# Rotary scores of latent attention in three reduced-precision products, and half-sized projection units in the sparse attention

## The chip, the cores and the metric

The program runs on one core of a Trainium2 chip. Times are device microseconds (us) from the start to the end of one execution. TensorE (PE, with its weight loads as PEld) does the matrix products, VectorE (DVE) and ScalarE (ACT) work on tiles of 128 partitions by 512 elements in on-chip memory, GpSimd (POOL) prepares weights, SyncE (SP) issues weight loads. The metric is the time of the whole program; lower is better.

## The reference

One input x (1 x 512 x 1024, float32) goes through two blocks. Only what the change touches is cut out here: the latent attention (MLA) of the first block and the sparse attention of the second.

```
q = (c_q @ w_uq).reshape(bsz, seq, 16, 128 + 64)          # MLA: c_q has 256 columns
q_rope = apply_rope(q[..., 128:], cos, sin)
k_rope = apply_rope(ckr[..., 256:], cos, sin)               # one for all heads
apply_rope: [x1 * cos - x2 * sin, x2 * cos + x1 * sin]      # halves of 32
s = einsum(q_nope, k_nope) + einsum(q_rope, k_rope); softmax(s * scale, causal) @ v

proj = h @ w_in                                             # second block
q_lat = einsum("bshd,hdc->bshc", q, w_uk)                   # 16 heads
att_lat = softmax(q_lat . c_kv * scale + bias, selected keys) @ c_kv
att = einsum("bshc,hdc->bshd", att_lat, w_uv)
xbc = silu(causal_depthwise_conv(xbc, w, b))                # 4 taps
z * silu(z); sigmoid(g_att), sigmoid(g_ssm)
```

## The kernel before, in words

Everything is held transposed: features on partitions, the 512 positions along the free axis. A projection is a sum over 128x128 weight blocks. For near-float32 precision at the fast rate each operand is split into a rounded part "hi" and a rest "lo" of type fp32r, and `product` (L505 to L512) issues three matmuls of 128x512: hi x hi, hi x lo, lo x hi. Plain f32 matmuls are used where no split was made. The weights come in 376 tiles of eight blocks each, in the order in which PE uses them. Per tile SP loads the raw tile, POOL loads a rounded copy (L439) and subtracts (`w_lo`, L457), both some tiles ahead, and PE tells by `slots_free` that it began a tile.

Each engine has its own program, written out in order; semaphores join them. There is no planner: the tables at the top of the file set the order.

**MLA.** `kv` computes four tiles of 128 features (two of latent, one of rotary keys, one of the same keys with the halves of 32 swapped). Then come "units", each one bank of PSUM (bank 6 or 7 in turn): `d` (query latent, 24 matmuls), and for each of four groups of four heads `k`, `v`, `q` (6 matmuls each, four of each kind) and `r`: four per group, two with rotary queries and two with the swapped ones. For a pair of heads DVE multiplies the one by the cosine and the other by the sine and adds (L2062, L2065, L2067). The first group's units run ahead of the loop. The loop has 64 items, one per head and block i of 128 queries, with (i+1) x 128 keys. Per step n PE makes the scores of item n (L950: nope part, f32, 128 rows; L951: rotary part, f32, 64 rows; L952: causal mask, fp32r), at n = 6, 10, ... the product of probabilities and values of a head (L964, f32), the transposes of item n-2 (L979), and then the next group's units that `GROUP_STEPS` gives for n mod 16. DVE takes the row maximum of item n (L2101, L2103), normalises item n-1 (L2108, L2110), then frees its units. ACT takes the exponential (L1454), copies transposes (L1462), and rounds head outputs (L1442). Scores use banks 0 to 2, transposes 3 and 4, head outputs 5.

**Sparse attention.** Again 64 items. PE makes scores (L1117 f32, L1118 to L1120 fp32r), head products (L1127), transposes (L1142), and in each step the units of `D_STEPS[n]`: 44 large projections of 24 matmuls each (4 `gs`, 16 `z`, 24 `xb`), and small ones: `ql` (next head's latent query, L1015) and `uv` (values of two heads, L1019). All of them take banks 6 and 7 in turn; a unit waits until the one two before it was read. An `xb` unit is a convolution: ACT writes the last tap (L1504), DVE adds three more (L2138) and, a unit later, multiplies with the tanh (L2151); `z` needs ACT's tanh (L1500) and one DVE step (L2131). DVE does this at the end of the same step n, before the row maximum of item n+1. Results are stored to DRAM ("spilled") and read back in the state-space stage that follows, which starts with transposes (L1203), `products` into bank 5 (L1189), and on ACT with a wait for all stores before the gate tiles are loaded (L1638); DVE multiplies with them (L2179) and then scales the next transposed tile (L2395).

The places that the diff touches:

## Time and profile before

| | |
|---|---|
| time, median of 3 runs (lowest, highest) | 2756.27 us (2754.8, 2764.29) |
| the profiled execution's own time | 2756.11 us |
| its span, first to last instruction | 2754.2 us |
| PE busy | 2622.4 us (95%), 11724 matmuls |
| DVE, ACT, POOL busy | 1467.7 us (53%), 657.5 us (24%), 1139.1 us (41%) |
| mean granted clock of TensorE | 0.978 of 2.4 GHz |
| weight traffic | 436.62 MB moved, 159 GB/s mean |

A matmul's duration includes its fill, and neighbours overlap: 128x512 fp32r matmuls show some 0.39 us each, but start every 0.23 us. So the cost of PE work is read from start to start, and "busy" counts nearly all of the span. MLA's loop runs from 769.5 to about 1004 us, the sparse attention's from 1626 to 2051 us, the state-space stage after that. The profile's own times are some 2 us under the time of the execution.

### The profile page before, as it was taken

The numbers are of one execution on the slowest core, as the hardware profiler recorded it, in microseconds if no ns is written. First come the engines' busy times: TensorE is split into PE (matmuls) and PEld (weight loads), VectorE is DVE, ScalarE is ACT, GpSimd is POOL, SyncE is SP. The second block draws the span as 40 slices with busy tenths as digits, with TensorE's granted clock in tenths as the row PEclk, the third lists the DMA queues.
The fourth block names the chain that finished last, engine by engine and source line by source line (L and its number), as shares of the span: only waits on it lengthen the run. The fifth ranks groups of instructions, "written<-read, shape, count | busy, mean of one in ns | idle before, by whom it ended". The sixth has DMA issues, their size and how long they took to land.

```text
span 2754.2 us, 31018 instructions
## 1 busy us (share of the span) xinstructions
PE 2622.4 (95%) x11724; PEld 2045.0 (74%) x11724; DVE 1467.7 (53%) x2001; ACT 657.5 (24%) x1289; POOL 1139.1 (41%) x764
## 2 busy tenths in 40 slices
PE   7999899999999999999999999999989998899998
PEld 6888688888766668888886676766666666688886
DVE  4754574464644434645556774454445777555511
ACT  2003430021323321201113213332222431222200
POOL 4333355555421125555554443333222224455554
PEclk9999999999989999999999999999999999999999
DMA  6333356555421225555654564444353535456564
GB/s 204 123 116 125 121 190 198 188 194 194 158 77 62 65 85 189 197 189 193 209 189 152 156 224 136 157 149 139 129 183 123 168 96 175 144 193 198 186 197 168
DMA packets 149049, 436.62 MB, mean 159 GB/s; under 512 B 14064, under 2 KB 18352, under 8 KB 148912
## 3 DMA queue, kind: packets, MB, share of 16 engines
q1 hardware_dynamic: 64224, 200.29, 24.7%
q0 software_dynamic: 67584, 201.35, 20.9%
q10 hardware_dynamic: 17104, 33.14, 3.5%
q8 instruction: 88, 1.44, 0.2%
q14 instruction: 49, 0.40, 0.0%
HBM read 417.90 MB, written 16.83 MB: 158 GB/s over the span
## 4 chain that ended last, share of the span: by engine, by line
issue 36%; PE 33%; POOL 24%; DVE 3%; DMA 2%; ACT 2%; DVEq 1%; ACTq 0%; POOLq 0%; SPq 0%
POOL w_lo L457 19%; PE bank L509 9%; PE bank L512 9%; PE bank L511 9%; POOL w_hi L439 5%; PE bank L710 2%; DMA projections<-spill_out 1%; PE bank L1127 1%; PE bank L784 1%; DMA residual<-x_in 0%; PE bank L787 0%; PE bank L786 0%; PE bank L1087 0%; DVE next_gained L2273 0%; PE bank L1117 0%
## 5 line engine op out<-in xcount | busy, mean ns | idle before, releaser
L457 POOL TENSOR_TENSOR w_lo<-w_raw,w_hi 128x1024 fp32r<-128x1024 f32 x376 | 905.7, 2409 | 14.8 <-DMA w_hi<-stream 6.5
L439 POOL DMA_DIRECT2D w_hi<-stream x376 | 227.2, 604 | 1582.7 <-PE bank L509 1413.8
L509 PE MATMUL bank<-x_hi,w_hi 128*128 128x512 f32 x1472 | 590.2, 401 | 26.0 <-POOL w_lo L457 13.0
L511 PE MATMUL bank<-x_lo,w_hi 128*128 128x512 f32 x1472 | 578.4, 393 | 0.0
L512 PE MATMUL bank<-x_hi,w_lo 128*128 128x512 f32 x1472 | 577.8, 393 | 0.0
L509 PEld LDWEIGHTS bank<-x_hi,w_hi 128*128 128x128 f32 x1472 | 279.6, 190 | 94.8 <-issue 20.4
L512 PEld LDWEIGHTS bank<-x_hi,w_lo 128*128 128x128 f32 x1472 | 279.4, 190 | 59.5
L511 PEld LDWEIGHTS bank<-x_lo,w_hi 128*128 128x128 f32 x1472 | 279.7, 190 | 57.8 <-issue 2.4
L2010 DVE TENSOR_TENSOR relu_sq<-relu 128x512 f32<-128x512 f32 x64 | 179.1, 2799 | 94.6 <-ACT relu L1404 94.6
L509 PE MATMUL bank<-hidden_hi,w_hi 128*128 128x512 f32 x512 | 199.2, 389 | 0.0
L511 PE MATMUL bank<-hidden_lo,w_hi 128*128 128x512 f32 x512 | 199.2, 389 | 0.0
L512 PE MATMUL bank<-hidden_hi,w_lo 128*128 128x512 f32 x512 | 199.2, 389 | 0.0
L1404 ACT ACTIVATE relu<-bank 128x512 f32<-128x512 f32 x64 | 38.3, 599 | 404.8 <-PE bank L512 404.8
L2138 DVE SCALAR_TENSOR_TENSOR conv_acc<-bank,half_conv,conv_acc 128x511 f32<-128x511 f32 (+2 forms) x72 | 53.9, 748 | 112.0 <-ACT conv_acc L1504 107.9
L511 PEld LDWEIGHTS bank<-hidden_lo,w_hi 128*128 128x128 f32 x512 | 96.1, 188 | 20.1
L509 PEld LDWEIGHTS bank<-hidden_hi,w_hi 128*128 128x128 f32 x512 | 96.1, 188 | 20.1
L512 PEld LDWEIGHTS bank<-hidden_hi,w_lo 128*128 128x128 f32 x512 | 96.1, 188 | 19.6
L509 PE MATMUL bank<-x_mlp_hi,w_hi 128*128 128x512 f32 x256 | 100.1, 391 | 0.6 <-POOL w_lo L457 0.6
L512 PE MATMUL bank<-x_mlp_hi,w_lo 128*128 128x512 f32 x256 | 99.6, 389 | 0.0
L511 PE MATMUL bank<-x_mlp_lo,w_hi 128*128 128x512 f32 x256 | 99.6, 389 | 0.0
L2483 DVE SCALAR_TENSOR_TENSOR ffn_val<-bank,consts,ffn_val 128x511 f32<-128x511 f32 (+1 forms) x44 | 33.0, 749 | 86.4 <-ACT ffn_val L1757 84.8
L2021 DVE TENSOR_TENSOR mlp_scaled<-bank,mlp_rstd 128x512 f32<-128x512 f32 x16 | 11.1, 692 | 110.0 <-PE bank L512 110.0
(434 smaller groups left out, 4448.4 us busy)
## 6 DMA issues: line engine op xcount, KB each, us to landing
w_hi<-stream POOLq DMA_DIRECT2D x376, 512.0 KB, 4.7
w_raw<-stream SPq DMA_DIRECT2D x376, 512.0 KB, 3.7
projections<-spill_out ACTq DMA_DIRECT2D x56, 256.0 KB, 2.0
ssm_x<-projections ACTq DMA_DIRECT2D x4, 1024.0 KB, 7.5
gate_tiles<-projections ACTq DMA_DIRECT2D x16, 256.0 KB, 3.6
ssm_z<-projections ACTq DMA_DIRECT2D x16, 256.0 KB, 2.7
residual<-x_in SPq DMA_DIRECT2D x4, 512.0 KB, 11.6
toeplitz_hi<-toeplitz_rows_hi POOLq DMA_DIRECT2D x4, 512.0 KB, 6.6
```

Of the source, the lines that this page charges most:

```text
L439: e.dma_start(in_slot(whi, t % SLOTS, o), in_stream(o)).then_inc(hi_ready[t % SLOTS], 16)
L457: e.tensor_tensor(wlo[:, s, :], raw[:, s, :], whi[:, s, :].bitcast(F32), ALU.subtract).then_inc(lo_ready, 1)
L509: mm = e.matmul(out, wh, rh, start=first, stop=False)
L511: e.matmul(out, wh, rl, start=False, stop=False)
L512: return e.matmul(out, wl, rh, start=False, stop=last)
L710: mm = e.matmul(o.rearrange("p (n l) -> p n l", l=L), hks[:, hh, chunk(c)], right, start=True, stop=True)
L784: mm = e.matmul(o, xh[:, k, chunk(t)], wh, start=k == 0, stop=False)
L1127: mm = e.matmul(bank[5][:, k * P:], dcn[:, k, :], mpt[:, k, k * P:], start=k == 0, stop=k == ST - 1)
L1404: e.activation(r_[:, j, :], bank[j][:, :], ACT.Relu).then_inc(f.free, 1)
L2010: tt(t_[:, j, :], r_[:, j, :], r_[:, j, :], ALU.mult)
L2138: mm = stt(a[:, lag:S], b[:, 0:S - lag], half_conv[:, 24 * k + m:24 * k + m + 1], a[:, lag:S], ALU.mult, ALU.add)
L2483: mm = stt(acc[:, lag:S], b[:, 0:S - lag], weights[:, 44 * k + t:44 * k + t + 1], acc[:, lag:S], ALU.mult, ALU.add)
```

## The change

In MLA the swapped weights are no longer used: `kv` has three tiles, and a group has two `r` units. DVE makes the swap itself by reading other partitions, in four operations on 32 partitions (`rotated`), adds, and the sum is split into hi (ACT) and lo (DVE). Keys are split likewise, once, with a mask so that each half of 64 partitions has its own pair of tiles whose other half is zero. The rotary score is three fp32r matmuls over 128 rows in place of one f32 matmul over 64. `GROUP_STEPS` changes.

In the sparse attention a large unit is issued in two halves of 12 matmuls (`half_unit`), spread over the steps by `D_PARTS`; DVE handles a unit one step after ACT. `ql` and `uv` move to bank 5, in an order given by `FIFTH`, and `products` waits until bank 5 was read. The last two large units are now convolutions, in steps 64 and 66; they were `z` units in steps 66 and 67.

```
-for _k, _u in enumerate(_mixed):
-    D_STEPS[_k * D_ITEMS // len(_mixed)].append(_u)
-D_STEPS[66].append(("z", 0, 14))
-D_STEPS[67].append(("z", 0, 15))
-for _h in range(1, 16):
-    D_STEPS[4 * _h - 3].append(("ql", 0, _h))
-for _t in range(8):
-    D_STEPS[8 * _t + 12].append(("uv", 0, _t))
+_halves = [(_u, _kh) for _u in _mixed for _kh in range(2)]
+for _n in range(D_ITEMS):
+    D_PARTS[_n] = [_halves.pop(0) for _ in range(2 if _n % 4 == 0 or _n % 16 == 11 else 1)]
+D_PARTS[D_ITEMS] = [_halves.pop(0) for _ in range(2)]
+D_PARTS[D_ITEMS + 2] = _halves
+for _n, _parts in enumerate(D_PARTS):
+    D_STEPS[_n] = [_u for _u, _kh in _parts if _kh]
+UV_AT = {8 * _t + (12 if _t < 7 else 11): _t for _t in range(8)}
+QL_AT = {4 * _h - 3: _h for _h in range(1, 16)}
...
+FIFTH = []
+for _n in range(len(D_STEPS)):
+    if _n >= 6 and _n % 4 == 2:
+        FIFTH.append(("out", _n // 4 - 1))
+    if _n in UV_AT:
+        FIFTH.append(("uv", UV_AT[_n]))
+    if _n in QL_AT:
+        FIFTH.append(("ql", QL_AT[_n]))
+FIFTH_AT = {_x: _n for _n, _x in enumerate(FIFTH)}
...
-        rp, kr = at("rope_table", 200, [P, 2, S]), at("mla_k_rope", 204, [P, S])
+        rp, rsum = at("rope_table", 200, [P, 2, S]), at("rope_sum", 130, [P, S])
+        krh = [at(f"mla_k_rope_hi{x}", kb, [P, S], F32R) for x, kb in enumerate((204, 134))]
+        krl = [at(f"mla_k_rope_lo{x}", kb, [P, S], F32R) for x, kb in enumerate((132, 136))]
...
-            UNITS += [(_k, 0, _j) for _j in range(4)]
-        GROUP_STEPS = {2: ["v0"], 3: ["v1"], 4: ["v2"], 5: ["v3"], 6: ["k0", "k1"], 7: ["k2", "k3"], 8: ["q0"],
-                       9: ["q1"], 10: ["q2"], 11: ["q3"], 12: ["r0", "r1"], 13: ["r2"], 14: ["r3"]}
+            UNITS += [(_k, 0, _j) for _j in range(2 if _k == "r" else 4)]
+        GROUP_STEPS = {3: ["v0"], 4: ["v1", "v2"], 5: ["v3"], 7: ["k0"], 8: ["k1", "k2"], 9: ["k3", "q0"], 11: ["q1"],
+                       12: ["q2", "q3"], 13: ["r0"], 15: ["r1"]}
...
-                        s, m = r_slot[0], (0, 2, 1, 3)[j]
+                        s = r_slot[0]
                         for k in range(2):
-                            b = slice((2 * m + k) * P, (2 * m + k + 1) * P)
+                            b = slice((2 * j + k) * P, (2 * j + k + 1) * P)
...
+                    if n % 8 == 0:
+                        e.wait_ge(rope_done, 2 + n // 8 + 1)
+                    if g and n % 16 == 0:
+                        e.wait_ge(un_act, 4 * (2 * g - 1))
                     if n >= 3:
                         e.wait_ge(at_e, n - 2)
                     b, w_ = bank[n % 3], (i + 1) * P
-                    r = slice(64 * (j % 2), 64 * (j % 2) + 64)
+                    x = rope_slot(n // 8)
+                    qh, ql, kh, kl = rqh[x][:, chunk(i)], rql[x][:, chunk(i)], krh[j % 2][:, 0:w_], krl[j % 2][:, 0:w_]
                     e.matmul(b[:, 0:w_], gq[g % 2][:, j, chunk(i)], gk[g % 2][:, j, 0:w_], start=True, stop=False)
-                    e.matmul(b[:, 0:w_], gr[g % 2][r, j // 2, chunk(i)], kr[r, 0:w_], start=False, stop=False)
+                    e.matmul(b[:, 0:w_], qh, kh, start=False, stop=False)
+                    e.matmul(b[:, 0:w_], ql, kh, start=False, stop=False)
+                    e.matmul(b[:, 0:w_], qh, kl, start=False, stop=False)
...
+            def half_unit(u, kh):
+
+                _, _, j = UNITS[u]
+                o = bank[6 + u % 2]
+                if kh == 0:
+                    a, d = freed_before(u - 1)
+                    if by_act(u - 2):
+                        e.wait_ge(un_act, a)
+                    else:
+                        e.wait_ge(un_dve, d)
+                for k in range(4 * kh, 4 * kh + 4):
+                    mm = product(e, w, o[:, :], xh2[:, k, :], xl2[:, k, :], k == 0, k == 7)
+                if kh:
+                    mm.then_inc(un_full, 1)
...
+                def head_values(t):
+                    e.wait_ge(at_oc, FIFTH_AT["uv", t])
+                    for q in range(2):
+                        mm = e.matmul(bank[5][64 * q:64 * q + 64, :], wuv[:, 2 * t + q, :], dlo[:, q, :],
+                                      start=True, stop=True)
+                    mm.then_inc(at_o, 1)
+
+                def next_query(hh):
+                    e.wait_ge(at_oc, FIFTH_AT["ql", hh])
+                    latent_query(bank[5][:, :], hh).then_inc(at_o, 1)
...
-                    for x in D_STEPS[n]:
-                        unit(UNIT_AT[x])
+                    if n in UV_AT:
+                        head_values(UV_AT[n])
+                    if n in QL_AT:
+                        next_query(QL_AT[n])
+                    for x, kh in D_PARTS[n]:
+                        half_unit(UNIT_AT[x], kh)
...
+                        e.wait_ge(at_oc, len(FIFTH))
                         products(0)
...
+                def rope_high(pair):
+                    e.wait_ge(rope_full, 1 + pair + 1)
+                    e.activation(rqh[rope_slot(pair)][:, :], rsum[:, :], ACT.Copy).then_inc(rope_hi, 1)
...
+                        rotated(rsum[:, :], rt[:, :], b).then_inc(un_dve, 1)
                         e.drain()
-                        tt(o, rt[:, :], o, ALU.add).then_inc(rope_done, 1)
-                        e.drain()
+                        tt(rsum[:, :], rt[:, :], rsum[:, :], ALU.add).then_inc(rope_full, 1)
+
+                def rotated(o, own, x):
+                    tt(own, x, rp[:, 0, :], ALU.mult)
+                    for q in range(4):
+                        a, b = slice(32 * q, 32 * q + 32), slice(32 * (q ^ 1), 32 * (q ^ 1) + 32)
+                        mm = tt(o[a], x[b], rp[b, 1, :], ALU.mult)
+                    return mm
+
+                def rope_low(pair):
+                    x = rope_slot(pair)
+                    e.wait_ge(rope_hi, 2 + pair + 1)
+                    tt(rql[x][:, :], rsum[:, :], rqh[x][:, :].bitcast(F32), ALU.subtract).then_inc(rope_done, 1)
+                    e.drain()
...
-                for u in range(6, 18):
+                for x in range(2):
+                    e.wait_ge(rope_hi, x + 1)
+                    stt(krl[x][:, :], krr[:, 1, :], own_half[:, x:x + 1], krh[x][:, :].bitcast(F32), ALU.mult,
+                        ALU.subtract).then_inc(rope_done, 1)
+                for u in range(6, 16):
                     unit(u)
+                    if u >= 14:
+                        rope_low(u - 14)
+                low_next = None
                 for n in range(MLA_ITEMS + 2):
                     if n < MLA_ITEMS:
...
-                    for x in D_STEPS[n]:
+                    if n in UV_AT:
+                        t = UV_AT[n]
+                        e.wait_ge(uv_hi, t + 1)
+                        tt(atl[:, t, :], bank[5][:, :], ath[:, t, :].bitcast(F32), ALU.subtract).then_inc(at_oc, 1)
+                        e.drain().then_inc(at_lo, 1)
+                    for x in (D_STEPS[n - 1] if n else []):
                         unit(UNIT_AT[x])
+                for x in D_STEPS[-1]:
+                    unit(UNIT_AT[x])
```

DVE in MLA's loop, second group's rotary units, before: the last product waits a step, and a rotary pair is three operations (`mla_o_lo` is a head output's lo part).

```order
L2062 TENSOR_TENSOR rope_tmp<-bank,rope_table 128x512
L2101 TENSOR_REDUCE mla_row_max<-bank 128x1
L2103 TENSOR_SCALAR mla_neg_max<-mla_row_max 128x1
L2108 RECIPROCAL mla_row_inv<-mla_row_sum 128x1
L2110 TENSOR_SCALAR mla_probs<-mla_probs,mla_row_inv 128x256
L2065 TENSOR_TENSOR mla_gq_rope_107<-bank,rope_table 128x512
L2067 TENSOR_TENSOR mla_gq_rope_107<-rope_tmp,mla_gq_rope_107 128x512
L2072 TENSOR_TENSOR mla_o_lo<-bank,mla_o_hi 128x512
```

After, at the same place (step 15 and 16):

```order
L2132 TENSOR_TENSOR rope_tmp<-bank,rope_table 128x512
L2135 TENSOR_TENSOR rope_sum<-bank,rope_table 32x512 x4
L2129 TENSOR_TENSOR rope_sum<-rope_tmp,rope_sum 128x512
L2186 TENSOR_REDUCE mla_row_max<-bank 128x1
L2188 TENSOR_SCALAR mla_neg_max<-mla_row_max 128x1
L2193 RECIPROCAL mla_row_inv<-mla_row_sum 128x1
L2195 TENSOR_SCALAR mla_probs<-mla_probs,mla_row_inv 128x512
L2141 TENSOR_TENSOR mla_rope_lo_111<-rope_sum,mla_rope_hi_108 128x512
```

What was spread over two steps as three operations of 128 partitions stands now in one block of six, ahead of the next row maximum, with a seventh behind it.

DVE from the last normalised item to the state-space stage (`ssm_x_nat`, `merged`), before:

```order
L2330 RECIPROCAL mla_row_inv<-mla_row_sum 128x1
L2332 TENSOR_SCALAR mla_probs<-mla_probs,mla_row_inv 128x512
L2131 SCALAR_TENSOR_TENSOR spill_out<-tanh_175,bank 128x512
L2151 SCALAR_TENSOR_TENSOR spill_out<-tanh_176,conv_acc 128x512
L2131 SCALAR_TENSOR_TENSOR spill_out<-tanh_176,bank 128x512
L2174 TENSOR_TENSOR att_lo<-bank,att_hi 128x512
L2395 TENSOR_TENSOR ssm_x_nat_196<-bank,ssm_dt 128x512
L2179 SCALAR_TENSOR_TENSOR merged<-gate_tiles,bank 128x512
```

After:

```order
L2228 SCALAR_TENSOR_TENSOR conv_acc<-bank,half_conv,conv_acc 128x509
L2241 SCALAR_TENSOR_TENSOR spill_out<-tanh_185,conv_acc 128x512
L2422 TENSOR_TENSOR att_lo<-bank,att_hi 128x512
L2228 SCALAR_TENSOR_TENSOR conv_acc<-bank,half_conv,conv_acc 128x511
L2228 SCALAR_TENSOR_TENSOR conv_acc<-bank,half_conv,conv_acc 128x510
L2228 SCALAR_TENSOR_TENSOR conv_acc<-bank,half_conv,conv_acc 128x509
L2241 SCALAR_TENSOR_TENSOR spill_out<-tanh_184,conv_acc 128x512
L2241 SCALAR_TENSOR_TENSOR spill_out<-tanh_185,conv_acc 128x512
L2488 TENSOR_TENSOR ssm_x_nat_205<-bank,ssm_dt 128x512
L2265 SCALAR_TENSOR_TENSOR merged<-gate_tiles,bank 128x512
```

The last operations ahead of `ssm_x_nat` were one each for two `z` units and a tanh product; now a convolution's three taps and two tanh products stand there, behind the last `att_lo`.

## Rows read from the trace of the kernel before

**Rows 1.** Busy time by stretch: span, engines' busy (count), clock, DMA.
```profile
1050.00:1100.00 50.00, 50.00 (x223) 41.39 (x221) 23.68 (x16) 7.50 (x11) 27.50 (x18) 1.00 0.60 189
...
770.90:794.80 23.90, 23.90 (x51) 11.92 (x50) 6.74 (x26) 5.76 (x19) 0.00 (x0) 0.50 0.00 0
...
1626.00:2051.00 425.00, 393.35 (x1724) 294.82 (x1724) 191.42 (x374) 124.61 (x300) 134.10 (x92) 0.97 0.45 145
```

**Rows 2.** PE's waits from 735 to 1010 us: total us, times, longest.
```profile
PE bank L893 <- DVE mla_gv L2058: 4.1, 1, 4.1
PE bank L979 <- DVE mla_probs L2110: 4.0, 7, 1.3
PE bank L950 <- DVE mla_gq_rope L2067: 1.6, 1, 1.6
```

**Rows 3.** PE's waits from 1626 to 2051 us.
```profile
PE bank L1142 <- DVE mla_probs L2332: 23.0, 10, 4.1
PE bank L1127 <- ACT mla_probs_t L1608: 6.6, 6, 3.2
```

**Rows 4.** Timeline of PE in MLA: start, duration, line, operation.
```profile
870.65 2.37 PE L964 MATMUL bank<-mla_probs_t,mla_gv 128*128 128x512 f32 x8
...
874.36 1.02 PE L950 MATMUL bank<-mla_gk,mla_gq 128*128 128x512 f32 x2
...
876.53 0.40 PE L979 MATMUL bank<-consts,mla_probs 128*128 128x128 f32 x2
876.69 0.48 PE L509 MATMUL bank<-mla_cq_hi,w_hi 128*128 128x512 f32 x1
877.01 0.39 PE L511 MATMUL bank<-mla_cq_lo,w_hi 128*128 128x512 f32 x1
...
878.17 0.38 PE L950 MATMUL bank<-mla_gk,mla_gq 128*128 128x128 f32 x2
...
879.06 0.51 PE L979 MATMUL bank<-consts,mla_probs 128*128 128x128 f32 x3
```

**Rows 5.** Timeline of PE in the sparse attention, no unit between.
```profile
1767.76 1.02 PE L1117 MATMUL bank<-dsa_c,dsa_qlat 128*128 128x512 f32 x2
...
1768.85 0.28 PE L1119 MATMUL bank<-toeplitz_hi,flip_r 128*128 128x256 f32 x1
...
1769.31 0.39 PE L1117 MATMUL bank<-dsa_c,dsa_qlat 128*128 128x128 f32 x2
...
1769.59 0.28 PE L1119 MATMUL bank<-toeplitz_hi,flip_r 128*128 128x128 f32 x1
1769.70 0.28 PE L1120 MATMUL bank<-toeplitz_lo,flip_r 128*128 128x128 f32 x1
```

**Rows 6.** DVE's groups of instructions by shape: busy us, mean ns.
```profile
L2249 DVE TENSOR_TENSOR ssm_acum_t_lo<-bank,ssm_acum_t_hi 32x512 fp32r<-32x512 f32 x1 | 0.7, 669 | 0.0
```

**Rows 7.** ACT's copy of a head output in MLA, same view.
```profile
L1442 ACT ACTIVATE mla_o_hi<-bank 128x512 fp32r<-128x512 f32 x16 | 9.5, 592 | 4.1 <-PE bank L964 4.1
```

**Rows 8.** Timeline of DVE, MLA's loop and the state-space stage.
```profile
876.73 0.69 DVE L2101 TENSOR_REDUCE mla_row_max<-bank 128x1 f32<-128x512 f32 x1 [0.88 <-PE bank L952]
...
877.80 0.42 DVE L2110 TENSOR_SCALAR mla_probs<-mla_probs,mla_row_inv 128x384 f32<-128x384 f32 x1
...
2085.34 1.29 DVE L2387 TENSOR_TENSOR ssm_g<-bank,ssm_g 128x512 f32<-128x512 f32 x2 [2.95 <-ACT ssm_g L1663]
```

**Rows 9.** Timeline: a DVE operation beside POOL's `w_lo`.
```profile
1999.34 2.87 DVE L2332 TENSOR_SCALAR mla_probs<-mla_probs,mla_row_inv 128x384 f32<-128x384 f32 x1
1999.57 2.40 POOL L457 TENSOR_TENSOR w_lo<-w_raw,w_hi 128x1024 fp32r<-128x1024 f32 x1
```

**Rows 10.** Timeline: end of the sparse attention and start of the state-space stage.
```profile
2050.96 1.08 PE L1019 MATMUL bank<-dsa_lat,dsa_wuv 128*64 128x512 f32 x4
...
2059.92 0.69 DVE L2179 SCALAR_TENSOR_TENSOR merged<-gate_tiles,bank 128x512 f32<-128x512 f32 x1 [5.61 <-DMA gate_tiles<-projections]
...
2061.49 0.66 PE L1203 MATMUL bank<-consts,ssm_x 128*128 128x128 f32 x4 [2.04 <-DVE ssm_x_nat L2395]
```

More of the change, by code:

```diff
@@ L85 @@
 D_ITEMS = 64
-D_STEPS = [[] for _ in range(D_ITEMS + 5)]
+D_STEPS = [[] for _ in range(D_ITEMS + 4)]
+D_PARTS = [[] for _ in D_STEPS]
 _others = [("gs", 0, m) for m in range(4, 8)] + [("z", 0, m) for m in range(16)]
@@ L146 @@
 for _g in (2, 3):
-    _x = [x for us in D_STEPS[16 * _g - 15:] for x in us if x[0] in SECTION][0]
+    _x = [x for parts in D_PARTS[16 * _g - 15:] for x, kh in parts if kh == 0][0]
     BIAS_AT[FETCH_AT[FIRST[SECTION[_x[0]]] + _x[2], None]] = [_g]
@@ L914, in mla @@
                 for kh in range(2):
-                    for m in range(4):
+                    for m in range(3):
                         if kh == 0:
-                            e.wait_ge(*(f.ring[m] if m < 4 else (f.free, f.f0 + m - 3)))
+                            e.wait_ge(*f.ring[m])
                         for k in range(4 * kh, 4 * kh + 4):
@@ L936, in mla @@
                 e.wait_ge(la_lo, 4)
-                for u in range(10, 18):
+                for u in range(10, 16):
                     unit(u)
@@ L996, in _, with latent_query @@
             mlp(1)
+            def latent_query(o, j):
+                r = slice(64 * (j % 2), 64 * (j % 2) + 64)
+                return e.matmul(o, wuk[r, j // 2, :], dq2[r, j // 2, :], start=True, stop=True)
+            def half_unit(u, kh):
[11 more added lines that the diff above has]
+                    mm.then_inc(un_full, 1)
             def unit(u):
@@ L1010, in unit @@
                 elif kind == "ql":
[L1011 to L1020 removed]
+                    e.wait_ge(extra_loaded, 16 * 5)
+                    e.wait_ge(un_act, freed_before(UNIT_AT["dq", 0, 7] + 1)[0])
+                    mm = latent_query(o[:, :], j)
                 elif kind == "ys":
@@ L1123, in out_product @@
                     e.wait_ge(at_c, n0 + 4 * hh + 4)
[L1124 to L1125 removed]
+                    e.wait_ge(at_oc, FIFTH_AT["out", hh])
                     for k in range(ST):
@@ L1447, in mla @@
                 latent(1, cq, cqh, rstd_q)
+                e.wait_ge(rope_full, 1)
+                for x in range(2):
+                    e.activation(krh[x][:, :], krr[:, 1, :], ACT.Copy, scale=own_half[:, x:x + 1]).then_inc(rope_hi, 1)
+                for pair in range(2):
+                    rope_high(pair)
                 for n in range(MLA_ITEMS + 2):
```

91 lines of the change are left out of this document (44 added, 47 removed), and 2 rows, old and new, of the table flow.

## The prediction

> **What bounds the kernel now.** I read the page first (PE busy 95%, the other engines at most 53%), then the stretches, then PE's waits in the two stages that change, then single steps in the timeline. The reader is to see that PE is the bound nearly everywhere, so two things count: PE's work, and the pauses and slow stretches of PE. In dense work a 128x512 matmul starts every 50 / 223 = 0.224 us at the full clock of 2.4 GHz [rows 1]. In MLA PE hardly waits inside the loop: 4.0 us in seven pauses, and in the run-up 4.1 and 1.6 us [rows 2]. But from 770.9 to 794.8 us, right behind the 1.6 us pause, the granted clock is 0.50, the 1.2 GHz level, while PE makes only scores, transposes and a head product; with the first dense units it is back [rows 1]. In the sparse attention PE waits 23.0 us for normalised rows, which DVE makes late because it had a convolution first, and 6.6 us for copied transposes [rows 3]; the mean clock there is 0.97 over 425 us [rows 1].
>
> **MLA, PE's work.** `kv` loses one tile of 24 matmuls, each group two `r` units of 6, in all 24 + 48 = 72, times 0.224 = -16.1 us [rows 1]. PE follows the chain of DVE there, but the first wait of that chain (`nx_sum`) is earlier than the work removed, so I count all of it. (If DVE held PE, 5 us of it would go.)
>
> A score item takes now 876.53 - 874.36 = 2.17 us at 512 keys and 879.06 - 878.17 = 0.89 at 128 [rows 4]; the widths between lie on a line, so a head costs 2 x (2.17 + 0.89) = 6.12. After: f32 plus one fp32r matmul take 1768.85 - 1767.76 = 1.09 at 512 and 1769.59 - 1769.31 = 0.28 at 128, a fp32r one 0.224 at 512 and 1769.70 - 1769.59 = 0.11 at 128 [rows 1, 5]. With two more fp32r and the mask (0.11) an item is 1.09 + 0.45 + 0.11 = 1.65 and 0.28 + 0.22 + 0.11 = 0.61, a head 4.52. That saves 1.6 per head, 16 heads, -25.6 us. The three matmuls cost less than the one since f32 takes about four times as long per column and the 64-row weights load in the open. The first seven items run at half clock, where the saving (seven quarters of 1.6 us) counts twice: -2.8 us. Bounds for the scores: -15 us, if only the f32 matmul goes and each fp32r one costs its width plus its weight load, to -31 us.
>
> **MLA, what DVE adds.** A `rotated` block is five products, a sum and the lo part. An operation on 32 partitions lasts 669 ns [rows 6], as long as one on 128: its price follows the free size. Back to back, two start 1.29 - 0.69 = 0.60 apart [rows 8]. So from the end of the `r` unit: 4 x 0.60 + 0.69, a drain of 0.1, the sum 0.69: 3.9 us; then ACT 0.59 [rows 7] and the lo part 0.69, with 0.1 for each hand-over: 5.4 us. In the run-up PE has for the first pair only the second `r` unit (6 x 0.224 = 1.35 us) to do, so it pauses 4.2 us where it was 1.6 [rows 2]: +2.6. The keys' two lo parts stand ahead of the values that release PE: 2 x 0.69, +1.4 behind the 4.1 us pause.
>
> In the loop the queue behind a `rotated` block is what hurts. Step 13 (`r0`) is followed by a head product of 2.2 us [rows 4] and two wide items, which cover it. Step 15 (`r1`) is followed by short work: items 0 and 1 of the next head, 0.6 and 0.9 us, with some 0.3 of transposes. DVE begins `r1` late, because row maximum, normalising and a head's lo part of step 14 came first: PE waits about 0.7 us in step 16. Then 3.9 us of rotation, and from row maximum to normalised row another 1.2 (at 512 wide it is 877.80 + 0.42 - 876.73 = 1.49 [rows 8]), while PE has 1.3 us: about 3.7 us of pause in step 17, and 0.8 for the copy behind it. 5.2 us a group, three groups: +15.6 us. Bounds: 0, if the operations overlap better, to 27, if the lo part counts too. In steps without dense work the shorter score also uncovers DVE's 1.49 us [rows 8]: +0.5 per head for four heads, +2.
>
> **MLA, the clock.** A pause of 1.6 us among f32 work was followed by 23.9 us at 0.50 [rows 1, 2]. The new 3.7 us pauses lie in steps 16 to 18 that have no dense units; the next is in step 19. I expect 5 to 7 us at half clock at each, 3 us lost, +9 for three. From 0 (no fall) to 30 (fall until the dense work of several steps has passed).
>
> Sum for MLA: -16.1 - 25.6 - 2.8 + 2.6 + 1.4 + 15.6 + 2 + 9 = -13.9 us.
>
> **Sparse attention.** No matmul goes. What goes is the pause: with half a unit (12 x 0.224 = 2.7 us) in every step and DVE a step later with the taps, the normalised row that PE transposes in step n is made before the convolution of step n-1, with some 8 us of PE work between. Of 23.0 + 6.6 us [rows 3] I leave 4 (a tail of 0.7, the rest where POOL stalls DVE): -25.6. The clock: 0.03 x 425 = 12.8 us' worth of ticks [rows 1], of which a few fall into pauses; I take -9. The 24 or so additional changes between kinds of matmul cost 877.01 - 876.69 - 0.224 = 0.1 us each [rows 4]: +2.5. `ql` and `uv` have each other's readers to wait for in bank 5, steps apart and behind a half unit: 0 to +4, taken 0.
>
> The seam to the state-space stage gets worse. Now `uv`, at 2050.96, is followed at 2059.92 by the first product with a gate tile and at 2061.49 by the transposes that wait for DVE behind it, a pause of 2.0 us [rows 10]. Afterwards `products` waits for ACT's and DVE's reading of bank 5 (0.6 + 0.7), and the last large unit is a convolution: three taps (2.4), tanh (0.6), the product (0.7), all behind `att_lo`, before its store, and the gate's load waits for that store on ACT. That moves 2059.92 by some 5.5 us. `products`, the dense unit and the first transposes cover none of it, since they are in the 2.0 us pause's calculation already: +5.5, and +2.5 for a fall of the clock in a pause of over 6 us. Bounds 2 and 14.
>
> Sum: -25.6 - 9 + 2.5 + 5.5 + 2.5 = -24.1 us. All: -38.0 from the profiled 2756.11, so 2718.1; the median 2756.27 lies 0.2 above the profile, and I say 2718.
>
> **A rule against the change.** A DVE operation that lasts 0.42 us elsewhere took 2.87 when POOL's 2.40 us `w_lo` began beside it [rows 8, 9]. The rotation's sums and lo parts read two tiles from on-chip memory; the products read PSUM. The Trainium skill, SBUF — State Buffer, section "Who interferes with whom", says that a DVE instruction with two SBUF inputs contends with a GpSimd instruction that reads SBUF, and that the one issued second is blocked until the other ends; the one row here is of a form with one tensor and a column, and it agrees in size.
>
> **The rivals.** (1) The port: POOL starts a `w_lo` about when a new weight tile is begun, and each group's `r0` begins one. If it fell on the sum or lo part of both blocks, 2 x 2.4 us for three groups and the run-up: +19, so 2737. Against it: the five products come first and last 3.1 us, longer than a `w_lo` of 2.40 [rows 9] that begins beside them, and each reads PSUM, as the 1.29 us pair does [rows 8]. By the skill's rule, too, they would pass beside it. (2) The new DVE blocks and half clock eat MLA's gain whole: the upper bounds of pauses and clock (27 and 30 in place of 15.6 and 9), MLA +18, total 2750; a milder form 2735. For it: MLA's DVE had no such block, and the 23.9 us row. (3) The pauses in MLA don't come (PE's work covers the blocks): 15.6 + 9 less, 2693. (4) The lag does not do what it says: the halves let PE reach a transpose sooner after a score, and DVE with stalls from POOL is late all the same; half of the 30 us stays with its clock, +18: 2736. (5) Slower: the clock falls in MLA and stays. Place: the loop from 795 to 1004 us; mechanism: pauses of over 3 us in work that, as the 23.9 us row shows, does not bring 2.4 GHz back; price: half of each us spent so. It decides from 2 x 52 us on, half of the loop, since 38 + 14 must be lost: 2775. Against it: dense units stand in ten of 16 steps, and with dense work the clock came back at once.
>
> **How the numbers follow.** Chances: forecast 0.48, (3) 0.17, (2) 0.15, (1) 0.09, (4) 0.07, (5) 0.04. 0.5% is 13.8 us, about what a measurement of this kernel can tell from no change. Faster than 2742.5 are the forecast, (3), (1), (4) nearly whole, and the milder half of (2): 0.87. Same 0.09, slower 0.04. The range from 2692 to 2741 takes in (3), (1), (4) and the milder (2), and leaves 0.15 out; the forecast's own is 2705 to 2730.
>
> **What would show it.** PE matmuls +56 (128 more, 72 fewer). MLA items of about 1.65 and 0.61 us. In MLA three pauses of 3 to 4 us before transposes (waiting for `mla_probs`) in the second step of each of the last three groups, with clock 0.50 behind them. In the sparse attention the waits of 23.0 and 6.6 us fall below 5 in sum, and the clock stays above 0.99. A pause of about 6 us before the second transposes of the state-space stage. Wrong would be: pauses left in the sparse attention, an operation on 32 partitions that lasts well off 0.67 us, or a fp32r matmul of 128 columns over 0.15 us.

## The result and the profile after

The change made the kernel faster: 2723.95 us (median of 4 runs, 2719.7 to 2730.51) against 2756.25 for the kernel before beside it. The ratio is 0.9878, with a 95% interval from 0.9865 to 0.9891: 33.6 us less by the ratio, 32.3 by the medians. The forecast was 2718. The profiled execution took 2719.7 (span 2717.9); it was the fastest of the four. The total fits, but not by the forecast's terms: MLA gave back nearly everything, the sparse attention gave more. First the two stages of the kernel before, by busy time between the same two instructions (first MLA score to first product with `mla_o_hi`; first sparse score to `products`); then the same of the changed kernel. Columns: stretch, its length, PE busy (count), PEld, DVE, ACT, POOL, mean granted clock, DMA share, GB/s.

```profile
769.51:1006.97 237.46, 232.76 (x897) 143.32 (x897) 100.77 (x301) 83.18 (x231) 35.45 (x24) 0.94 0.17 54
1626.14:2052.46 426.32, 394.81 (x1730) 295.47 (x1731) 192.11 (x375) 125.49 (x301) 134.10 (x92) 0.97 0.44 145
```

```profile
767.66:1005.00 237.34, 203.41 (x924) 155.01 (x925) 135.47 (x332) 87.11 (x238) 35.23 (x24) 0.91 0.17 54
1623.25:2013.19 389.94, 383.14 (x1731) 290.82 (x1731) 173.13 (x371) 124.89 (x300) 133.64 (x92) 1.00 0.49 159
```

MLA's loop lasts as long as before, though PE is busy 29 us less in it. Length less busy is idle: 4.7 us before, 33.9 after. Busy multiplied by the clock is the work at 2.4 GHz, to some 2 us, since the clock has two digits: 219 before, 185 after. So 34 us of work went, 29 us of pauses and 4 us of half clock came. In the sparse attention the work is some 383 us in both; 24.7 us of pauses went, and busy time fell by 11.7, to all appearance the slow clock's.

PE's waits of the changed kernel, first from 700 to 1010 us (they answer to [rows 2]), then from 1626 to 2051 (to [rows 3]): total us, times, longest.

```profile
PE bank L1001 <- DVE mla_probs L2195: 32.8, 21, 4.0
PE bank L910 <- DVE mla_gv L2123: 5.4, 1, 5.4
PE bank L970 <- DVE mla_rope_lo L2141: 4.4, 1, 4.4
PE bank L522 <- POOL w_lo L470: 1.9, 2, 1.0
...
PE bank L1254 <- DVE ssm_x_nat L2488: 6.1, 2, 5.3
PE bank L1189 <- DVE mla_probs L2418: 3.3, 6, 0.6
...
PE bank L1163 <- ACT mla_probs_t L1666: 1.4, 1, 1.4
```

MLA's transposes wait for normalised rows 21 times, 32.8 us, where it was 4.0 in seven; the sparse ones 3.3 where it was 23.0. Now the timeline of one group's turn in MLA, in order of time; in brackets what the engine idled before the row, and for whom.

```profile
822.15 0.69 DVE L2132 TENSOR_TENSOR rope_tmp<-bank,rope_table 128x512 f32<-128x512 f32 x1
...
822.85 2.79 DVE L2135 TENSOR_TENSOR rope_sum<-bank,rope_table 32x512 f32<-32x512 f32 x4
...
825.73 0.69 DVE L2129 TENSOR_TENSOR rope_sum<-rope_tmp,rope_sum 128x512 f32<-128x512 f32 x1
...
827.12 0.49 DVE L2195 TENSOR_SCALAR mla_probs<-mla_probs,mla_row_inv 128x512 f32<-128x512 f32 x1
...
827.66 1.11 PE L1001 MATMUL bank<-consts,mla_probs 128*128 128x128 f32 x4 [3.98 <-DVE mla_probs L2195]
...
834.18 1.02 PE L970 MATMUL bank<-mla_gk,mla_gq 128*128 128x512 f32 x2
...
835.80 0.39 PE L1001 MATMUL bank<-consts,mla_probs 128*128 128x128 f32 x2
...
837.07 2.83 DVE L2195 TENSOR_SCALAR mla_probs<-mla_probs,mla_row_inv 128x384 f32<-128x384 f32 x1
...
837.31 2.36 POOL L470 TENSOR_TENSOR w_lo<-w_raw,w_hi 128x1024 fp32r<-128x1024 f32 x1
...
839.96 0.55 PE L1001 MATMUL bank<-consts,mla_probs 128*128 128x128 f32 x3 [1.76 <-DVE mla_probs L2195]
```

The rotation takes 4.27 us, and PE pauses 3.98 behind it, as forecast (3.7). A score item of 512 keys takes 835.80 - 834.18 = 1.62 us (forecast 1.65, before 2.17 [rows 4]). What the forecast did not have is the last part: a normalising that [rows 8] show at 0.42 us takes 2.83 beside POOL's `w_lo`, and PE pauses 1.76 us. That happens six times in MLA (791.47, 839.96, 855.09, 901.69, 916.82 and 965.76 us). A third thing that no term of the forecast names stands at the loop's start: the second pair's rotation lies ahead of the loop's first row maxima, and PE pauses 2.72 us.

```profile
772.68 0.69 DVE L2141 TENSOR_TENSOR mla_rope_lo<-rope_sum,mla_rope_hi 128x512 fp32r<-128x512 f32 x1 [0.70 <-ACT mla_rope_hi L1498]
773.46 0.29 DVE L2186 TENSOR_REDUCE mla_row_max<-bank 128x1 f32<-128x128 f32 x1
...
775.09 0.48 PE L1001 MATMUL bank<-consts,mla_probs 128*128 128x128 f32 x1 [2.72 <-DVE mla_probs L2195]
```

The long normalising never came in MLA before; one line's own view of each kernel shows the longest of 64 at 491 ns before and at 2835 ns after (min, median, max):

```profile
L2110 DVE TENSOR_SCALAR mla_probs<-mla_probs,mla_row_inv x64: 285/387/491, 773.7 to 1001.4; 128x128 f32<-128x128 f32 x16, 128x256 f32<-128x256 f32 x16, 128x384 f32<-128x384 f32 x16, 128x512 f32<-128x512 f32 x16
```

```profile
L2195 DVE TENSOR_SCALAR mla_probs<-mla_probs,mla_row_inv x64: 285/386/2835, 774.8 to 998.8; 128x128 f32<-128x128 f32 x16, 128x256 f32<-128x256 f32 x16, 128x384 f32<-128x384 f32 x16, 128x512 f32<-128x512 f32 x16
```

The cause was looked for in `GROUP_STEPS`: the tiles of `v` and `k` are now begun in steps 3 and 7 of a group, where DVE normalises 384 columns at the moment when POOL starts on the next tile. The experiment with the units one to a step tries this.

### The profile page after: what moved, and what is told of

It is laid out like the page before. It is cut to its first block, busy times and chain, and to the rows that moved or that the text cites. A ratio compares the mean times of both kernels' runs of the same rounds, so it can differ in the third digit from the quotient of the medians.

```text
span 2717.9 us, 31048 instructions
## 1 busy us (share of the span) xinstructions
PE 2571.4 (95%) x11716; PEld 2044.5 (75%) x11716; DVE 1495.3 (55%) x2046; ACT 663.1 (24%) x1299; POOL 1134.9 (42%) x764
## 4 chain that ended last, share of the span: by engine, by line
issue 35%; PE 33%; POOL 24%; DVE 4%; DMA 2%; ACT 2%; DVEq 1%; ACTq 0%; POOLq 0%; SPq 0%
POOL w_lo L470 19%; PE bank L522 9%; PE bank L525 8%; PE bank L524 8%; POOL w_hi L452 5%; PE bank L727 2%; DMA projections<-spill_out 1%; PE bank L1154 1%; PE bank L1163 1%; DMA residual<-x_in 1%; PE bank L801 1%; PE bank L804 0%; PE bank L803 0%; PE bank L1121 0%; DVE next_gained L2359 0%
## 5 line engine op out<-in xcount | busy, mean ns | idle before, releaser
L522 PE MATMUL bank<-x_hi,w_hi 128*128 128x512 f32 x1464 | 587.8, 402 | 28.8 <-POOL w_lo L470 15.3
L522 PEld LDWEIGHTS bank<-x_hi,w_hi 128*128 128x128 f32 x1464 | 276.7, 189 | 113.8 <-issue 40.4
L522 PE MATMUL bank<-hidden_hi,w_hi 128*128 128x512 f32 x512 | 199.3, 389 | 0.0
L2409 DVE TENSOR_REDUCE mla_row_max<-bank 128x1 f32<-128x128 f32 (+1 forms) x64 | 31.4, 491 | 183.4 <-PE bank L1157 182.5
L522 PEld LDWEIGHTS bank<-hidden_hi,w_hi 128*128 128x128 f32 x512 | 96.2, 188 | 19.8
L522 PE MATMUL bank<-x_mlp_hi,w_hi 128*128 128x512 f32 x256 | 100.2, 391 | 0.6 <-POOL w_lo L470 0.6
```

The lines of the kernel that those rows point to most:

```text
L522: mm = e.matmul(out, wh, rh, start=first, stop=False)
L2409: e.reduce_max(mmx[:, n:n + 1], bank[n % 3][:, 0:wd], axis=AX.X)
```

## The experiments

Times are compared with runs of the kernel before on the same chip, in five rounds each. Executions of one kernel differ by some us, so where a few us matter I read the same stretch in both profiles.

**Each half alone.** The kernel before with only the MLA edits, and with only the sparse edits.

> The kernel before with the MLA half of the change alone (rotary scores in hi and lo, kv with three tiles, two r units, new group steps); the sparse attention is the old one. Theory A (MLA's matmul work did shrink by some 40 us, but PE pauses behind DVE and half clock give nearly all of it back): 1 to 5 us faster than before, 2752 to 2755; MLA shows the same pauses as in the changed kernel (three of 4.0 us, six of 1.76 us), the sparse attention its old pauses of 30 us. Rival B (the MLA half alone gains some 14 us, as forecast, and the traces of before and after differ by luck of the clock): 2742. Rival C (it has no effect on the rest but the halves of the change work together): time outside the sum of the two parts by over 5 us.

> The kernel before with the sparse half of the change alone (halved units, DVE's taps a step later, uv and ql in the fifth bank). Theory A (nearly the whole gain is here): 29 to 32 us faster, 2724 to 2727, with pauses of about 7 us in the stage and one of 5.3 us at the seam. Rival B (sparse part gains the 24 forecast): 2732. The two halves' gains should sum to that of the whole change within 3 us.

MLA alone: 2764.68 us, ratio 1.0027 (1.0016 to 1.0038), slower by 4 to 10 us. Sparse alone: 2727.02, 0.9888 (0.9873 to 0.9903), 31 us faster. So all of the gain is the sparse half's, and theory A holds for the two stages: in the first kernel MLA's loop lasts 237.38 us with the very pauses of the changed kernel, and its sparse stage has the old ones.

```profile
766.98:1004.36 237.38, 203.46 (x924) 154.87 (x925) 135.42 (x332) 87.21 (x238) 35.22 (x24) 0.91 0.17 54
1627.09:2055.67 428.58, 396.78 (x1731) 297.38 (x1731) 192.51 (x375) 125.31 (x301) 133.98 (x92) 0.97 0.44 144
```

But the two do not sum to the whole within the 3 us expected: +7.4 - 30.9 = -23.5 us, and the whole change has -33.6, so rival C's sign (off by over 5 us) came. Theory A expected MLA alone 1 to 5 us faster, which is a miss. Its profiled execution, 2756.99 us, was the fastest of its seven, so the profile doesn't show what the median holds. These 10 us stay open. The profiles show one thing that can make such differences without any edit: stages whose code is the same differ by some us from profile to profile, with the granted clock. The part behind the first product with `ssm_xd` in the changed kernel, and in the second kernel of the last group of experiments:

```profile
2036.93:2717.89 680.96, 637.26 (x2906) 494.39 (x2906) 373.90 (x464) 170.59 (x328) 291.17 (x192) 0.98 0.52 165
```

```profile
2012.40:2698.15 685.75, 642.36 (x2906) 497.14 (x2906) 374.03 (x464) 170.57 (x328) 291.84 (x192) 0.97 0.51 164
```

So a stage is compared with the same stage, and a few us of the total are not laid to an edit.

**The rotation block of `r1` a step later on DVE, and its hi part a step later on ACT.** PE makes the unit where it did. DVE's edit (ACT's is of the same kind):

```
-  for u in STEP_UNITS[n]:                      # DVE, end of step n
+  for u in (r1 of STEP_UNITS[n - 1]) + (STEP_UNITS[n] without r1):
```

> The changed kernel with one thing moved in MLA: the rotation block of each group's second r unit is made by DVE one step later, behind the normalising of item 15 of the group (and ACT's hi part of it a step later). Same instructions. Theory A (the 3.98 us pause in the group's step 17 is the rotation block of 4.3 us standing ahead of the normalising): the three pauses fall below 1.5 us each and the half clock behind them goes: 3 x (2.5 to 4) + 3 x 2 = 12 to 18 us faster than the changed kernel, about 2708. Rival B (the block only moves: the next transposes wait as long, as head product and one item do not cover it): no gain, 2720 to 2725. Rival D (clock gives nothing back, since 0.5 us pauses and the 1.76 us ones keep it low): 8 to 10 us, 2714.

2728.29 us, ratio 0.9894 (0.9879 to 0.9909): no gain. Rival B's mechanism is right; the time lies 3 us above its range. PE's, DVE's and ACT's timeline around a group's start:

```profile
826.50 2.79 DVE L2138 TENSOR_TENSOR rope_sum<-bank,rope_table 32x512 f32<-32x512 f32 x4
...
829.38 0.69 DVE L2132 TENSOR_TENSOR rope_sum<-rope_tmp,rope_sum 128x512 f32<-128x512 f32 x1
...
830.11 0.63 ACT L1498 ACTIVATE mla_rope_hi<-rope_sum 128x512 fp32r<-128x512 f32 x1 [3.99 <-DVE rope_sum L2132]
...
830.79 0.47 ACT L1515 ACTIVATE mla_probs<-bank,mla_neg_max 128x256 f32<-128x256 f32 x1
...
831.26 0.59 ACT L1523 ACTIVATE mla_probs_t<-bank 128x512 f32<-128x512 f32 x1
...
831.90 2.02 PE L986 MATMUL bank<-mla_probs_t,mla_gv 128*128 128x512 f32 x2 [3.94 <-ACT mla_probs_t L1523]
```

The transposes no longer wait, but ACT's hi part of the rotated row waits for DVE, and behind it in ACT's queue stands the copy that the head product needs. The pause of 3.98 us became one of 3.94. (An expectation further down says that the block was moved on DVE alone; ACT's part was moved with it.)

**Units one to a step.** Here only the table differs:

```
-  {3: [v0], 4: [v1, v2], 5: [v3], 7: [k0], 8: [k1, k2], 9: [k3, q0], 11: [q1], 12: [q2, q3], 13: [r0], 15: [r1]}
+  {2: [v0], 3: [v1], 4: [v2], 5: [v3], 6: [k0], 7: [k1], 8: [k2], 9: [k3], 10: [q0], 11: [q1], 12: [q2, q3], 13: [r0], 15: [r1]}
```

> The changed kernel with MLA's dense units placed one to a step from step 2 on, so that the weight tiles of v, k and q are begun in steps 2, 6 and 10 of a group in place of 3, 7 and 9; r0 and r1 stay at 13 and 15. Same instructions. Theory A (the 1.76 us pauses are DVE's normalising of 384 columns, blocked for 2.4 us by POOL's lo part of a tile begun in the same step): all six go with the six blocked rows of 2.83 us, 10.6 us of pause and 1 to 4 us of clock less; single units in steps 4 and 8 may bring up to 0.7 us each back (4.5 us): 2710 to 2718. Rival B (the pauses come from the short distance between score and transposes in steps 4 and 8 and have nothing to do with POOL): they stay or grow, since those steps now have half the dense work: 2722 to 2735.

2707.86 us, ratio 0.9822 (0.9808 to 0.9835), 16 us below the changed kernel. All six blocked rows and all six pauses of 1.76 us are gone, and no other pause came; that is theory A, and 2 us more than its range:

```profile
769.96:990.88 220.92, 197.57 (x924) 150.97 (x925) 120.76 (x332) 87.06 (x238) 35.50 (x24) 0.93 0.18 58
```

```profile
L2195 DVE TENSOR_SCALAR mla_probs<-mla_probs,mla_row_inv x64: 285/386/491, 777.0 to 984.5; 128x128 f32<-128x128 f32 x16, 128x256 f32<-128x256 f32 x16, 128x384 f32<-128x384 f32 x16, 128x512 f32<-128x512 f32 x16
```

The loop is 237.34 - 220.92 = 16.4 us shorter: idle 33.9 to 23.3, which is six times 1.76, and the rest is clock. This settles POOL's `w_lo` beside the normalising as the cause, with DVE as the one that waits. The runs show the wait, and not the place where the two meet; that it is a port is the reading given further down.

**The second `r` unit in the next group's step 1**, in addition to the table above:

```
-  15: [r1]
+  1: [r1 of this group, not of the next]
```

> The kernel with units one to a step (v, k, q begun in steps 2, 6, 10 of a group), and here each group's second r unit is moved, on PE, ACT and DVE alike, from step 15 to step 1 of the next group, in front of a head product and a dense unit; it is needed only eight items into the group. In the changed kernel with the block one step later on DVE alone, the pause of 3.98 us had turned into one of 3.94 us of the head product for ACT's copied transposes, since ACT's hi part of the rotated row waits ahead of that copy. Theory A (a rotation block needs some 5.4 us of PE work between it and the transposes or product that come next, whichever engine's queue they stand in; step 1 has 1.2 + 2.2 + 1.3 + 1.6 us): the three pauses of 3.98 us go and nothing over 1 us takes their place; 9 to 12 us of pause and up to 6 of half clock less than with the units one to a step: 2690 to 2699. Rival B (the pause moves a second time, to the copy or the head product of step 18): 2704 to 2708.

2700.91 us, ratio 0.9802 (0.9788 to 0.9815). The loop lasts 213.05 us (220.92 with r1 in step 15). The three pauses of 3.98 us are gone; apart from the 2.7 us at the loop's start, PE's longest are now 1.50 us. Idle is 18.0 us against 23.3. The time lies between theory A's range and rival B's. Theory A's direction holds, but it promised 9 to 12 us of pause and I got 5.3: 1.50 us appear in step 16 of a group, where no dense unit is left ahead, and 0.7 and 0.3 behind the unit's new place.

**The sparse half, taken apart.** Without the lag; with whole units (42 over 64 steps; the expectation's 38 is wrong); and with neither, so that the fifth bank stays, and with it the two convolutions at the end.

```
no lag:        -  for x in D_STEPS[n - 1]: unit(x)     +  for x in D_STEPS[n]: unit(x)
whole units:   -  D_PARTS[n] = one or two halves       +  D_PARTS[k * 64 // 42] += both halves of unit k
```

> The changed kernel, but DVE makes the taps of a sparse-attention unit in the step in which PE ends it, not one step later; halves stay. Theory A (the lag is what takes the normalising out from behind the taps; the halves only spread the work): the normalised rows are late again in steps with a convolution, 12 to 24 pauses of 0.5 to 1.5 us: 10 to 20 us slower than the changed kernel, 2734 to 2744. Rival B (the halves alone do it, since half a unit of PE work stands in every step, and the lag is of no account): 2720 to 2727.

> The changed kernel with the sparse attention's dense units whole again (38 whole units over 64 steps, one or none to a step, as before; the last two are convolutions in steps 64 and 66), with the lag and the fifth bank kept. Theory A (the lag does most; whole units leave steps with no dense work, where DVE's row maximum and normalising, 1.5 us, and its stalls by POOL are uncovered): pauses of 12 to 20 us in place of 6.8: 5 to 13 us slower, 2729 to 2737. Rival B (the halves do it all, the lag nothing): the old pauses come back, 25 to 30 us: 2745 or more.

> The changed kernel with both the lag and the halves undone in the sparse attention: whole units, taps in the step in which PE ends the unit; only uv and ql in the fifth bank stay of that half of the change. The runs so far: halves without the lag have the same 0.55 us pauses as the changed kernel, whole units with the lag 0.85 us ones. Theory A (either of the two is enough, since each puts a half or a whole unit of PE work, 2.7 to 5.4 us, between the taps and the transposes that need the row behind them): with neither, the old pauses of 1.5 to 4 us come back, 20 to 30 us in the stage with its clock: 2745 to 2756. Rival B (the fifth bank did it: uv and ql no longer stand in the ring of two banks behind the taps, and lag and halves add little): pauses of 8 to 13 us, 2725 to 2735.

No lag: 2724.30 us, ratio 0.9878 (0.9862 to 0.9893), the same as with it. Whole units: 2733.41, 0.9917 (0.9903 to 0.9930). Neither: 2778.98, 1.0080 (1.0065 to 1.0096), slower than the kernel before by 22 us. The stage up to `products` in that order of kernels, one fence each:

```profile
1628.81:2021.30 392.49, 384.51 (x1730) 291.86 (x1730) 194.81 (x375) 124.58 (x301) 133.65 (x92) 1.00 0.48 158
```

```profile
1623.66:2017.52 393.86, 384.88 (x1730) 291.88 (x1730) 187.71 (x371) 124.85 (x300) 134.11 (x92) 1.00 0.47 157
```

```profile
1622.80:2069.05 446.25, 405.38 (x1730) 303.82 (x1730) 185.20 (x375) 124.94 (x301) 133.88 (x92) 0.95 0.42 139
```

389.9 with both, 392.5 and 393.9 with one, 446.3 with neither: against the old pauses either edit is enough. Theory A of the first of these runs, that the lag does the work, fell. The whole units came out in theory A's range, 9 us above the changed kernel, but with 9.0 us of idle time in the stage in place of the 12 to 20 expected; the profiles put 4 us in the stage, 1 in the seam and 5 in the last, unchanged stage, so what the halves are worth beside the lag is between 4 and 9 us. Theory A of the last run held, and my price for it was too low. DVE's normalising is blocked by POOL even more often without the lag (20 rows, 8 with it; 25 and 11 with the products with a tanh), but the half unit in each step covers it. The kernel to compare the last run with is the MLA-only one, which has the same MLA and the old sparse attention (2764.68 us, stage 428.6). Why the kernel with neither is 14 us slower than that (idle time of the stage 40.9 us for 31.8) stands in its waits, and in ACT's and DVE's timeline before the longest wait for `dsa_qlat`:

```profile
PE bank L1188 <- DVE mla_probs L2417: 23.8, 11, 4.0
PE bank L1162 <- ACT dsa_qlat L1680: 7.7, 5, 2.6
PE bank L1162 <- ACT mla_probs_t L1665: 4.3, 2, 2.9
```

```profile
1857.26 2.40 DVE L2227 SCALAR_TENSOR_TENSOR conv_acc<-bank,half_conv,conv_acc 128x511 f32<-128x511 f32 x3 [1.89 <-ACT conv_acc L1566]
...
1860.84 0.47 ACT L1657 ACTIVATE mla_probs<-bank,mla_neg_max 128x256 f32<-128x256 f32 x1 [3.61 <-DVE mla_neg_max L2410]
...
1861.78 0.60 ACT L1680 ACTIVATE dsa_qlat<-bank 128x512 f32<-128x512 f32 x1
```

The old 23 us are back, and the head product in bank 5 now waits too for ACT's reading of `ql`, which stands in ACT's queue behind exponentials that wait for DVE's taps. The fifth bank alone, with the new end, is a loss; the halves or the lag pay for it.

**Two `z` units last.**

```
+  for _z in (14, 15): _mixed.remove(("z", 0, _z)); _mixed.append(("z", 0, _z))
```

> The changed kernel with the order of the sparse attention's dense units changed at its end: the two z units 14 and 15 come last in place of two convolutions (as before the change), so that the last unit needs one tanh and one product of DVE and no taps. Theory A (the 5.3 us pause before the state-space stage's transposes is the taps of the last convolution, which stand behind the last head's lo part and ahead of the store that the gate's load waits for): the pause falls to 2 to 3 us: 2 to 4 us faster, 2716 to 2722. Rival B (the wait is for products that need bank 5's readers, and the order of units is of no account): 2721 to 2726 and a pause of 5 us.

2724.49 us, ratio 0.9884 (0.9869 to 0.9899): by the total nothing. The place itself: the pause at the second transposes is 2.39 us (first row below), it was 5.31 (the rows of the changed kernel behind it).

```profile
2031.55 0.66 PE L1257 MATMUL bank<-consts,ssm_x 128*128 128x128 f32 x4 [2.39 <-DVE ssm_x_nat L2491]
```

```profile
2013.19 1.16 PE L1240 MATMUL bank<-ssm_c,ssm_b 128*128 128x128 f32 x8 [1.00 <-DVE att_lo L2422]
...
2025.66 0.69 PE L1254 MATMUL bank<-consts,ssm_x 128*128 128x128 f32 x2 [5.31 <-DVE ssm_x_nat L2488]
```

From the first sparse score to the first product with `ssm_xd` it took 409.9 us, 413.7 in the changed kernel. So theory A's 2 to 4 us are there in the profile, and too small for the runs to show; by the time alone rival B would have passed.

**Together.** Units one to a step with the late r1, z units last, and the keys' two lo parts behind the values' copies; the same without the lag; and the last with the keys' lo parts ahead again.

> Three edits of the changed kernel together: MLA's units one to a step with the second r unit in step 1 of the next group; two z units last in the sparse attention; and in MLA's run-up the keys' two lo parts behind the values' copies in place of ahead of them. Theory A (gains add up, measured between the same instructions of the profiles): -21 for MLA's loop, -3.8 for the seam, -1.3 for the run-up, from 2724: 2696 to 2700. Rival B (the run-up's second pause grows by what the first loses, and the half clock stays where it was): 2699 to 2703.

> As the kernel with the three edits (units one to a step with the late second r unit, z units last, keys' lo parts later), and without the lag of the taps in the sparse attention. Theory A (with halves the lag is of no account inside the stage, and at the seam its absence takes the last unit's work out from behind the last lo part): the same time within 2 us, or 1 to 2 us faster. Rival B (DVE's rows blocked by POOL, 20 of them without the lag as against 11 with it, meet shorter cover somewhere): 2 to 6 us slower.

> As the kernel with three edits and without the lag, but the keys' two lo parts in MLA's run-up stand ahead of the values' copies again. The two kernels with them behind had in the run-up 4.05 + 2.64 + 4.40 + 1.72 = 12.8 us of pauses against 5.38 + 4.40 + 2.73 = 12.5 with them ahead, and a half-clock stretch of 13.7 us at the loop's start against two of 3.4. Theory A (the edit is worth nothing in pauses and costs some 3 us of clock): 2 to 4 us faster than that kernel's 2695.3, 2691 to 2694. Rival B (the clock stretch was luck): 2694 to 2697.

2697.71 us (0.9784, 0.9770 to 0.9798), 2695.32 (0.9771, 0.9755 to 0.9786) and 2696.03 (0.9779, 0.9763 to 0.9796). All three beat both kernels, the last two by 28 us on the changed one; they can't be told from each other. The first lies in theory A's range, the second is 2.4 us faster than the first where theory A had 1 to 2, and the third lies in rival B's range. Moving the keys' lo parts was worth nothing; the run-up of the first of the three shows why:

```profile
PE bank L973 <- DVE mla_rope_lo L2144: 4.4, 1, 4.4
PE bank L913 <- DVE mla_gv L2126: 4.0, 1, 4.0
PE bank L525 <- DVE mla_gq L2128: 2.6, 1, 2.6
```

The pause ahead of the values fell from 5.4 to 4.0, and a new one of 2.6 us stands behind the moved work. The clock's part of theory A in the last run is not confirmed by the time.

## Why the prediction was right, and where not

- **MLA's work.** Forecast for the loop: 36 dense matmuls (8.1) and the scores (25.6), 33.7 us. Measured: 219 to 185. Right to within what the clock's two digits show (some 2 us), and the wide item is too (1.62 for 1.65). The sign "PE matmuls +56" did not come: the pages count 11724 before and 11716 after. An f32 matmul has two records in the trace (the row at 834.18 is one matmul, x2), so an item's one for three is +1 and not +2, and 64 - 72 = -8.
- **`kv`.** 24 matmuls fewer were to give 5.4 us and gave about 3: PE now waits 1.9 us for POOL's `w_lo` (row L522 above), since every second of its weight tiles now has only four blocks that are used (`w.skip(4)` in the kernel). PE is through four blocks in 2.7 us (12 x 0.224), and POOL needs 0.58 + 2.40 for its load and subtraction. I had asked DVE's chain about this and not POOL's.
- **The run-up.** +1.4 and +2.6 forecast; 4.1 and 1.6 us [rows 2] became 5.4 and 4.4: +1.3 and +2.8. Right, though the forecast's own 5.4 - 1.35 gives a pause of 4.05 and not 4.2. Missing was a third pause, the 2.72 us behind the second pair.
- **The groups' pauses.** 3.7 forecast, 3.98 measured, for the reason given; two of 0.53 beside it for the 0.7. The four shifted products start 0.70 us apart where I took 0.60 from a pair on the same partitions [rows 8]. The Trainium skill, VectorE: DVE Perf Modes, section "Two Vector instructions with no wait between them", says that an instruction whose operand begins in another group of 32 partitions than the one before it starts only when all earlier ones have ended; the trace agrees, four in 2.79 us.
- **The port: the step that failed.** Rival (1) asked whether POOL's `w_lo` would fall on the rotation. It never stretched that: `w_lo` lay beside the products, without effect, and never beside a sum or lo part of the rotation (all 16 of these rows last 0.68 to 0.69 us), so the rule on two inputs was not tried there. It fell on the normalising, six times, 10.6 us of pause, a term that the sum held at nothing, and the experiment with the units one to a step gave it back with some 5 us of clock. I had the row [rows 9] and looked only at what the change adds, not at what the new table puts beside the old work. MLA was to give -13.9 and gave -2.5 from the first `kv` matmul on. By the Trainium skill, SBUF — State Buffer, section "Who interferes with whom", a `tensor_scalar` can enter a mode that takes both port pairs, and then contends with GpSimd; that sentence, and not the one on two inputs that I used, bears on these rows, and the trace agrees with it (2.83 us for 0.42).
- **MLA's clock.** 5 to 7 us at 0.50 behind each long pause forecast; measured 6.8 (826.0 to 832.8 us: 0.50). The loss in the loop grew by 4.3 us, forecast 6.2 (9 - 2.8). That the two are near is luck: the first 23.9 us at half clock went, which the forecast had only as a cheaper stretch, and short slow stretches came behind the pauses that it didn't have.
- **The rivals.** In the loop 29.2 us of pauses and 4.3 of clock ate 33.5 of the 33.7 us of work. That MLA's gain is eaten whole is rival (2), to which I gave 0.15, at a third of its price (11 us worse than the forecast, not 32) and in part through the port. The total came out as forecast because the sparse attention gave more.
- **Sparse pauses.** 29.6 to 4 forecast, 31.5 to 6.8 measured: -24.7 for -25.6. The reason was put wrongly: halves with lag, where either alone does nearly all of it.
- **Sparse clock and switches.** -9 forecast, and +2.5 for switches between kinds of matmul; busy time fell by 11.7 for these -6.5. No slow clock is left (1.00), and of the switches nothing is seen. These 5 us are the larger part of what the stage gained beyond the forecast.
- **The seam.** From `products` to the first product with `ssm_xd`: 18.3 us before, 23.7 after. Of these 5.5, 3.3 are pause (5.3 + 0.8 for 2.0 + 0.8) and the rest slower clock; `products` itself waits 1.0. So 4.3 for the 5.5 of pause forecast (the 1.0 stands among the stage's 6.8 too), and 2.2 for the 2.5 of clock. That the taps are the cause, as forecast, the run with two `z` units last bears out.

In sum, measured after less before: +0.5 at the start, MLA -2.5, between the stages -0.9, sparse and seam -30.9, behind them -2.5, -36.3 of span. The forecast had -13.9 and -24.1. Two errors, of +11 and -7, stood against each other, and the -0.9 and -2.5 lie in stages that the change doesn't touch, where profiles differ by the clock. So the nearness of the total, 2724 for 2718, is in good part luck.

## What to carry to other kernels

When a change moves work in time, list not only what it adds but each old instruction that comes to lie beside another engine's: here a table of steps put two tile starts next to a DVE operation, which cost 16 us. A block on one engine needs its cover ahead of every queue that waits for it; moved on DVE and ACT but not on PE, it took the pause from the transposes to the head product, and moved on all three with cover behind it, most of the pause went. Where two edits are made against one stall, take each away alone: here either was nearly enough, and the third edit without them was a loss of 14 us. Where two halves of a change don't touch each other, still add up their terms apart: here a total near the forecast hid two misses.

## What was not expected of the hardware

- The blocked DVE rows start 0.24 us before POOL's (837.07 and 837.31), and still DVE is the one that waits, 2.41 us, while `w_lo` keeps its 2.36. So which of the two waits, which the prediction puts down to the order of issue, can't be read from the starts of the rows.
- In the two attention stages, DVE's row maxima, taps and shifted products, which have an operand in PSUM, were never stretched beside `w_lo` in either profile.
- A pause of 1.76 us was followed by half clock in three of six cases: 3.4 us of it at 791.9, 918.2 and 966.0 us, and none around 839.96, 855.09 or 901.69.

```profile
826.00:832.80 6.80, 5.14 (x13) 3.50 (x14) 4.09 (x14) 3.11 (x9) 0.00 (x0) 0.50 0.00 0
837.00:847.00 10.00, 8.24 (x47) 6.95 (x45) 4.68 (x9) 5.18 (x13) 2.65 (x2) 1.00 0.33 107
853.00:863.00 10.00, 8.25 (x43) 6.76 (x43) 4.46 (x10) 4.31 (x11) 3.15 (x3) 1.00 0.36 109
918.20:921.60 3.40, 3.40 (x10) 2.64 (x9) 0.00 (x0) 0.60 (x1) 0.00 (x0) 0.51 0.00 0
```
